# Down product of a gated feed-forward block: seven block products in place of eight, three parts, block sums on GpSimd

## The chip, the cores and the metric

The kernel runs on one core of a Trainium2 chip. Five engines work from queues of their own: PE (TensorE, matmuls), DVE (VectorE), ACT (ScalarE), POOL (GpSimd) and SP (which issues most transfers). The metric is the device time of one execution in microseconds.

## The reference

Two layers of a hybrid diffusion step over 640 tokens (128 of context, 512 latent), width 1024. The change touches only the feed-forward block that ends each layer:

```python
def conv_ffn(h, p):
    u = h @ p['w_up']
    t = u.shape[1]
    pad = CONV_WIDTH // 2
    up = jnp.pad(u, ((0, 0), (pad, pad), (0, 0)))
    w = p['conv_w']
    u = up[:, 0:t] * w[0] + up[:, 1:t + 1] * w[1] + up[:, 2:t + 2] * w[2] + p['conv_b']
    a, gt = u[..., :D_FF], u[..., D_FF:]
    return (a * jax.nn.silu(gt)) @ p['w_down']
...
    x = x + gate_f * conv_ffn(h, p)
```

`w_up` is 1024 x 5632 and `w_down` is 2816 x 1024, all in float32.

## The kernel before

Activations lie with features on the 128 partitions and the 640 tokens along the free dimension, as two halves of 320 columns (`HALF`). Every float32 operand is split in two fp32r numbers: ACT copies it to the high half (`whi` for weights, `hhi`, `ahi` for activations), and a subtraction gives the low half (`wlo`, `hlo`, `alo`). A product takes three passes of matmuls: high by high, high by low, low by high. A tile of 128 output features is therefore 3 x 2 matmuls of 128x320 for each 128 input features.

One plan, `build_plan`, is a list of steps in program order. Each engine walks the same list (`walk`) and emits the steps that concern it, so a step's place in the list is its place in the queue of every engine that takes part. An engine never passes a step that waits. Semaphores such as `hi_ready`, `lo_ready`, `sub_done` and `fm_read` join the engines, and what is counted in them is worked out by `look_back` and `signals`.

Weights come by DMA into one of two slots of `raw` (`load_unit`), ACT makes the high half (`split`, line 1699), DVE the low half (line 2054), and PE multiplies (`feature_tile`, line 1376). There is room for two blocks of `SUB` = 1024 columns in `whi` and `wlo`.

The 22 tiles of the hidden width are done in two parts (`FPARTS`), of 12 and 10. In a part, the up units come first: unit a makes one tile of the value half and one of the gate half, 96 matmuls. Its results go through `up_out` (ACT reads both from PSUM into `va`, `vg`; DVE adds the two outer taps of the convolution, lines 2287 and 2294), and `up_out2`: silu on ACT, product on POOL (line 2367), high half `ahi` on ACT (line 1900), low half `alo` on POOL (line 2370). The queue order in the loop is: first weight block of unit a, `up_out` of unit a-1, first up matmuls, second weight block, `up_out2` of unit a-1, second up matmuls.

Then the down units follow: unit a is one tile of 128 output features, 6 or 5 hidden tiles in each of two blocks of weights, and `down_out` adds the gated result into `xT`, the residual stream (`residual`, line 2243). In the second part of layer 0, ACT also squares `xT` and DVE adds the squares up for the next layer's norm (line 2260). Up units and down units are both hardware loops.

## Time and profile before

| | |
|---|---|
| median of 3 runs | 2582.42 us (2577.47 to 2582.90) |
| profiled execution: its own time | 2577.76 us |
| its span | 2575.1 us |
| PE busy | 2479.7 us, 96% |
| DVE busy | 1370.1 us, 53% |
| ACT busy | 972.6 us, 38% |
| POOL busy | 410.5 us, 16% |

The span goes from the first instruction to the last. A busy share is an average over stages with different limits: the mixers are bound in other ways than the feed-forward block. A row names the line of the kernel, the engine, the operation, and the tile written and the tiles read. Where an engine was idle before a row, square brackets say how long and whose event ended it.

### The profile page before, as it was taken

What the parts mean: (1) busy time and instruction counts of PE and PEld (TensorE: products, weight loads), DVE (VectorE), ACT (ScalarE), POOL (GpSimd) and SP (SyncE); (2) the same over time, 40 slices, a digit from 0 to 9 for tenths busy, and PEclk for the clock granted to TensorE, in tenths of its full rate; (3) what the DMA queues carried; (4) which work ended last, traced back from release to release, by engine and by line L of the source; (5) the groups of instructions that cost most, each with busy time, mean ns of one, the idle gap of its engine ahead of it and who ended that gap; (6) DMA issues with size and microseconds to landing.
All of it is one profiled execution on the core that took longest, in us unless ns stands there. A gap on an engine that the chain in (4) does not pass through costs nothing.

```text
span 2575.1 us, 42771 instructions
## 1 busy us (share of the span) xinstructions
PE 2479.7 (96%) x17115; PEld 2257.8 (88%) x17115; DVE 1370.1 (53%) x2339; ACT 972.6 (38%) x1713; POOL 410.5 (16%) x362
## 2 busy tenths in 40 slices
PE   7999999999999999999999999999999999999998
PEld 5878977798799999999977799668978999999998
DVE  4674366646755454245447734766476555433542
ACT  5453255424533433133244523454244243322332
POOL 0500022023020221022004001220320202200220
PEclk8999999999999999999999999999999999999999
DMA  7312222422042222322332022222210422222222
GB/s 240 98 34 66 60 96 93 132 87 60 19 124 73 66 65 78 86 66 69 103 97 74 18 74 65 93 85 72 79 50 18 132 65 68 75 74 78 80 59 82
DMA packets 252833, 202.80 MB, mean 79 GB/s; under 512 B 9876, under 2 KB 235910, under 8 KB 252678
## 3 DMA queue, kind: packets, MB, share of 16 engines
q1 hardware_dynamic: 245574, 197.67, 25.4%
q10 hardware_dynamic: 7104, 2.95, 0.4%
q8 instruction: 111, 1.82, 0.3%
q14 instruction: 44, 0.36, 0.0%
HBM read 196.50 MB, written 4.10 MB: 78 GB/s over the span
## 4 chain that ended last, share of the span: by engine, by line
PE 88%; ACT 4%; DVE 4%; issue 1%; DMA 1%; SPq 1%; POOL 0%; ACTq 0%; POOLq 0%; DVEq 0%
PE ps L1376 48%; PE ps L1398 8%; PE ps L1547 6%; PE ps L1561 4%; PE ps L1588 4%; PE ps L1361 3%; PE ps L1363 3%; PE ps L1362 3%; ACT prob L1832 2%; PE ps L1488 1%; PE ps L1445 1%; PE ps L1251 1%; PE ps L1505 1%; PE ps L1508 1%; PE ps L1261 1%
## 5 line engine op out<-in xcount | busy, mean ns | idle before, releaser
L2054 DVE TENSOR_TENSOR wlo<-raw,whi 128x1024 fp32r<-128x1024 f32 (+4 forms) x284 | 357.5, 1259 | 434.1 <-ACT whi L1699 432.6
L1376 PE MATMUL ps<-hhi,whi 128*128 128x320 f32 x1856 | 425.2, 310 | 7.5 <-DVE wlo L2054 3.8
L1376 PE MATMUL ps<-hhi,wlo 128*128 128x320 f32 x1856 | 423.5, 309 | 0.0
L1376 PE MATMUL ps<-hlo,whi 128*128 128x320 f32 x1856 | 423.5, 309 | 0.0
L1699 ACT ACTIVATE whi<-raw 128x1024 fp32r<-128x1024 f32 (+4 forms) x284 | 277.7, 978 | 379.0 <-PE ps L1376 294.9
L1376 PEld LDWEIGHTS ps<-hhi,whi 128*128 128x128 f32 x1856 | 310.6, 188 | 9.8 <-DVE wlo L2054 5.1
L1376 PEld LDWEIGHTS ps<-hlo,whi 128*128 128x128 f32 x1856 | 311.0, 188 | 0.0
L1376 PEld LDWEIGHTS ps<-hhi,wlo 128*128 128x128 f32 x1856 | 310.8, 188 | 0.0
L2343 POOL TENSOR_TENSOR rstd<-smean,mhalf 128x4 f32<-128x4 f32 (+3 forms) x96 | 118.7, 1239 | 550.8 <-DVE smean L2104 550.1
L2128 DVE TENSOR_REDUCE negmax<-ps 128x1 f32<-128x640 f32 x192 | 151.8, 821 | 71.7 <-PE ps L1547 70.7
L1398 PE MATMUL ps<-hhi,whi 128*128 128x320 f32 x512 | 177.8, 347 | 0.5 <-issue 0.5
L2367 POOL TENSOR_TENSOR va<-va,vg 128x640 f32<-128x640 f32 x44 | 74.8, 1699 | 636.8 <-ACT vg L1898 636.8
L1832 ACT ACTIVATE prob<-ps,negmax 128x640 f32<-128x640 f32 x192 | 150.5, 792 | 67.2 <-DVE negmax L2128 67.2
L1376 PE MATMUL ps<-ahi,whi 128*128 128x320 f32 x704 | 160.6, 308 | 4.6 <-DVE wlo L2054 3.9
L1376 PE MATMUL ps<-alo,whi 128*128 128x320 f32 x704 | 159.9, 308 | 0.0
L1376 PE MATMUL ps<-ahi,wlo 128*128 128x320 f32 x704 | 159.8, 307 | 0.0
L1398 PE MATMUL ps<-hhi,wlo 128*128 128x320 f32 x512 | 159.2, 311 | 0.0
L1398 PE MATMUL ps<-hlo,whi 128*128 128x320 f32 x512 | 159.1, 311 | 0.0
L1842 ACT ACTIVATE probT<-ps 128x512 f32<-128x512 f32 (+1 forms) x172 | 88.2, 513 | 179.6 <-PE ps L1561 179.6
L1361 PE MATMUL ps<-whi,hhi 128*128 128x512 f32 (+2 forms) x400 | 146.3, 366 | 1.1 <-ACT vC L1736 0.9
L1363 PE MATMUL ps<-whi,hlo 128*128 128x512 f32 (+2 forms) x400 | 144.5, 361 | 0.0
L1362 PE MATMUL ps<-wlo,hhi 128*128 128x512 f32 (+2 forms) x400 | 144.0, 360 | 0.0
(248 smaller groups left out, 4335.9 us busy)
## 6 DMA issues: line engine op xcount, KB each, us to landing
raw<-in_w_up SPq DMA_DIRECT2D x88, 512.0 KB, 4.9
raw<-in_w_in SPq DMA_DIRECT2D x40, 1024.0 KB, 5.2
raw<-in_w_ada SPq DMA_DIRECT2D x29, 1024.0 KB, 5.2
raw<-in_w_down SPq DMA_DIRECT2D x16, 768.0 KB, 4.8
raw<-in_w_down SPq DMA_DIRECT2D x16, 640.0 KB, 4.4
adaw<-in_w_ada SPq DMA_DIRECT2D x8, 1024.0 KB, 11.4
raw<-in_w_o SPq DMA_DIRECT2D x8, 1024.0 KB, 5.5
raw<-in_w_branch_a SPq DMA_DIRECT2D x4, 1024.0 KB, 5.0
```

The lines of the kernel that those rows point to most:

```text
L1361: pe.matmul(out, hhi[:, kt, c], wh, start=kt == 0, stop=False)
L1362: pe.matmul(out, hhi[:, kt, c], wl, start=False, stop=False)
L1363: mm = pe.matmul(out, hlo[:, kt, c], wh, start=False, stop=kt == KD - 1)
L1376: mm = pe.matmul(out, w[:, sub, c], m[:, kt, o:o + HALF], start=first and i == 0 and a == 0, stop=last and i == len(ks) - 1 and a == 2)
L1398: mm = pe.matmul(bank(6)[:, OFF:], w[:, s["sub"], c], m[:, kt, o:o + HALF], start=kt == a == 0, stop=kt == KD - 1 and a == 2)
L1547: mm = pe.matmul(out, qt[:, q * P:(q + 1) * P], kt[:, SEQ + c:SEQ + c + HALF], start=True, stop=True)
L1561: mm = pe.transpose(bank(bk)[:, i * P:(i + 1) * P], src, ident[:, :])
L1699: act.activation(dst(whi), src, ACT.Copy).then_inc(S["hi_ready"], 1)
L1832: act.activation(prob[:, slot + m, :], run(m), ACT.Exp, bias=negmax[:, at], accum_out=sums)\
L2054: dve.tensor_tensor(dst(wlo), src, dst(whi).bitcast(F32), ALU.subtract).then_inc(S["lo_ready"], 1)
L2128: dve.tensor_reduce(negmax[:, slot + m:slot + m + 1], run(m), AX.X, ALU.max, negate=True)\
L2343: pool.tensor_tensor(rstd[:, par, 0:heads], smean[:, par, 0:heads], mhalf[:, 0:heads], ALU.pow)\
```

## The change

Part one: `FPARTS` becomes three parts, of 8, 8 and 6 hidden tiles. Part two: the down product of a part is worked out by Strassen's scheme in Winograd's form, on blocks. A column pair u is 256 output features: its weights are four blocks, A11 and A12 (the first output tile), A21 and A22 (the second), with the first and the second half of the part's hidden tiles. The tokens are in two halves as before. Seven products P1 to P7 replace eight. They take four weight blocks as they are and four block sums, S1 = A21 + A22, S2 = S1 - A11, S3 = A22 - S2 and S4 = A12 - S2 (A11, A12 and A22 serve as they are, A21 only in sums); POOL makes the sums in place in `raw` (`wmix`). On the activation side also, three block sums are made once for a part: `up_out3` takes the place of the end of `up_out2`. It makes high halves on ACT, low halves on DVE, and sums on POOL. An even unit has two copies of 320 columns and one sum, an odd unit two of 640 and one of 320, with two sums. All go to `acts`, which holds seven operands.

Part three: the results. Each product has a PSUM bank of its own for 320 columns, and DVE adds it with the gate straight into the quarters of `xT` that it belongs to (x11, x12 for the first output tile's token halves, x21, x22 for the second's). P1 is copied by ACT to a shared sum in `vg`, to which DVE adds P6 and later P7. Weight blocks are split in quarters of 512 columns (`qsplit`), four products ahead. The steps are written out, no longer in a loop.

```diff
-FPARTS = [(0, 12), (12, 10)]
+FPARTS = [(0, 8), (8, 8), (16, 6)]
+PAIRS = KD // 2
+PRODUCTS = ["P1", "P5", "P2", "P6", "P3", "P7", "P4"]
+WEIGHT = dict(P1="A11", P5="S1", P2="A12", P6="S2", P3="S4", P7="S3", P4="A22")
+PLACE = dict(A11=(0, 0), S3=(0, 0), A21=(0, 1), S1=(0, 1), S2=(0, 1), A12=(1, 0), S4=(1, 0), A22=(1, 1))
+READS = dict(P1=["x11"], P5=["x22", "x12"], P2=["x11"], P6=["U", "x12"], P3=["x12"], P7=["U", "x21", "x22"], P4=["x21"])
+OPERAND = dict(P1=0, P5=1, P2=2, P3=3, P6=4, P7=5, P4=6)
...
+        def load(u):
+            plan.append(dict(step="unit", src="down", slot=u % 2, a=u, of=l, **k))
+
+        def mix(u, name):
+            plan.append(dict(step="wmix", name=name, slot=u % 2, u=u, **k))
...
+        def split(g):
+            u, p = seq[g]
+            name = WEIGHT[p]
+            if name == "A11" and u > 1:
+                mix(u, "S1")
+            plan.append(dict(step="qsplit", name=name, u=u, slot=u % 2, q=g % 4, last=p == "P4", **k))
+            if name == "S1" and u:
+                mix(u, "S2")
+            if name == "A12" and u:
+                mix(u, "S4")
+                mix(u, "S3")
+            if name == "A22" and u + 2 < PAIRS:
+                load(u + 2)
...
+        def product(g):
+            u, p = seq[g]
+            need = 2 + (g > 1) if g < 4 else 1 if g < 8 else ends[g - 8]
+            plan.append(dict(step="prod", p=p, u=u, q=g % 4, bank=(g + 4) % 8, read_back=len(reads) - need,
+                             copy_back=sum(x > g - 8 for x in copies), **k))
...
+        out_v, out_g = [dict(last[2], a=nf - 1, s=1, js=js) for js in ((0,), (1,))]
+        plan.extend(last[:5])
+        load(0)
+        load(1)
+        plan.extend(last[5:7])
+        split(0)
+        mix(0, "S1")
+        plan.append(out_v)
+        split(1)
+        mix(1, "S1")
+        mix(0, "S2")
+        plan.append(last[7])
+        plan.append(out_g)
+        split(2)
+        split(3)
+        adds = []
+        for g in range(len(seq)):
+            u, p = seq[g]
+            product(g)
+            if g == 0:
+                plan.append(dict(last[5], a=nf - 1, s=1))
+            left = [read(g)]
...
+            if squares and p in ("P3", "P4"):
+                left.append(dict(step="down_sq", f=2 * u + (p == "P4"), **k))
+                adds.append(dict(step="down_sq2", f=2 * u + (p == "P4"), **k))
...
+            if g + 4 < len(seq):
+                split(g + 4)
+            if g == 1:
+                plan.append(dict(last[6], a=nf - 1, s=1))
+                mix(0, "S4")
+                mix(0, "S3")
...
+        def mixed(s, out, turn):
+
+            at = ds(turn + s["a"] // 2, 1)
+            a, b = va[:, 0, :].rearrange("p (o c) -> p o c", o=2), va[:, 1, :].rearrange("p (o c) -> p o c", o=2)
+            pieces = [(2, 4, b), (4, 6, a), (6, 7, b[:, 0:1, :])] if s["a"] % 2 else [(0, 1, a[:, 0:1, :]), (1, 2, a[:, 0:1, :])]
+            return [(out[:, i:j, at, :], x.unsqueeze(2)) for i, j, x in pieces]
...
+                def prod(s):
+
+                    p, half = s["p"], s["nf"] // 2
                     sub_waits(s)
-                    half = s["nf"] // 2
-                    if s["first"] and s["sub"] == 0:
-                        pe.wait_ge(S["alo_ready"], n("alo_ready", -half))
-                    fm_waits(s, 1)
-                    feature_tile(2 * s["s"], s["sub"], range(s["sub"] * half, (s["sub"] + 1) * half), P, 0, ahi, alo,
-                                 first=s["sub"] == 0, last=s["sub"] == 1, base=s["sub"] * half,
-                                 made="alo_ready" if s["first"] and s["sub"] else None).then_inc(S["sub_done"], 1)
+                    pe.wait_ge(S["fm_read"], n("fm_read", -s["read_back"]))
+                    pe.wait_ge(S["copy_done"], n("copy_done", -s["copy_back"]))
+                    out, (ah, al) = bank(s["bank"], HALF), operands(s)
+                    wh, wl = quarter(whi, s), quarter(wlo, s)
+                    for k in range(half):
+                        if s["u"] == 0 and k == half - 1:
+                            pe.wait_ge(S["alo_ready"], n("alo_ready", -dict(P1=1, P2=2, P3=2, P6=1, P7=1).get(p, 0)))
+                        c = slice(k * P, (k + 1) * P)
+                        for w, m, a in ((wh, ah, 0), (wh, al, 1), (wl, ah, 2)):
+                            mm = pe.matmul(out, w[:, c], m[:, OPERAND[p], k, :], start=k == a == 0, stop=k == half - 1 and a == 2)
+                    mm.then_inc(S["sub_done"], 1)
...
+                def down_sq(s):
+                    squares(s["f"], s["f"] % 2, -1)
+
+                def down_read(s):
+                    if s["p"] == "P1":
+                        act.wait_ge(S["sub_done"], n("sub_done"))
+                        act.wait_ge(S["fm_read"], n("fm_read", -s["room_back"]))
+                        act.wait_ge(S["prod_ready"], n("prod_ready", -int(s["u"] < 2)))
+                        act.activation(shared_sum(s), bank(s["bank"], HALF), ACT.Copy).then_inc(S["copy_done"], 1)
+
+                def qsplit(s):
+                    if s["name"][0] == "S":
+                        act.wait_ge(S["wmix_ready"], n("wmix_ready", -s["mix_back"]))
+                    else:
+                        act.wait_ge(S[f"raw_full{s['slot']}"], n(f"raw_full{s['slot']}"))
+                    act.wait_ge(S["sub_done"], n("sub_done", s["ahead"] - 1))
+                    act.activation(quarter(whi, s).rearrange("p (k c) -> p k c", c=P), block_of(s, s["name"]), ACT.Copy).then_inc(S["hi_ready"], 1)
...
+                def up_out3(s):
+
+                    act.wait_ge(S["prod_ready"], n("prod_ready"))
+                    for i, (out, src) in enumerate(mixed(s, operands(s)[0], n.turn)):
+                        if i:
+                            act.wait_ge(S["tmix_ready"], n("tmix_ready", i))
+                        act.activation(out, src, ACT.Copy).then_inc(S["ahi_ready"], 1)
...
+                    dve.wait_ge(S["hi_ready"], n("hi_ready", 1))
+                    wh, wl = [quarter(x, s).rearrange("p (k c) -> p k c", c=P) for x in (whi, wlo)]
+                    dve.tensor_tensor(wl, block_of(s, s["name"]), wh.bitcast(F32), ALU.subtract).then_inc(S["lo_ready"], 1)
+
+                def up_out3(s):
+                    ah, al = operands(s)
+                    for i, ((hi, _), (lo, src)) in enumerate(zip(mixed(s, ah, n.turn), mixed(s, al, n.turn))):
+                        dve.wait_ge(S["ahi_ready"], n("ahi_ready", i + 1))
+                        dve.tensor_tensor(lo, src, hi.bitcast(F32), ALU.subtract).then_inc(S["alo_ready"], 1)
...
+                    out = bank(s["bank"], HALF)
+                    total = shared_sum(s)
+                    for i, (op, back) in enumerate(s["ops"]):
+                        if back is not None:
+                            dve.wait_ge(S["fm_read"], n("fm_read", back))
+                        if op == "U":
+                            ins = dve.tensor_tensor(total, total, out, ALU.add)
+                        else:
+                            f, half = 2 * s["u"] + int(op[1]) - 1, int(op[2]) - 1
+                            src = total if p in ("P1", "P6", "P7") else out
+                            for j, (a, b) in enumerate(((0, SEQ), (SEQ, HALF))) if half == 0 else ((1, (HALF, T)),):
+                                x = xT[:, f, a:b]
+                                ins = dve.scalar_tensor_tensor(out=x, in0=src[:, a - half * HALF:b - half * HALF],
+                                                               scalar=mod[:, s["l"], 5 * KD + f, j:j + 1], in1=x,
+                                                               op0=ALU.mult, op1=ALU.add)
+                        ins.then_inc(S["fm_read"], 1)
 
...
-                    pool.wait_ge(S["ahi_ready"], n("ahi_ready", 1))
-                    u = ds(n.turn * 2 + s["a"], 1)
-                    pool.tensor_tensor(alo[:, u, :], a.unsqueeze(1), ahi[:, u, :].bitcast(F32), ALU.subtract)\
-                        .then_inc(S["alo_ready"], 1)
...
+                    if s["a"] % 2 == 0:
+                        pool.wait_ge(S["alo_ready"], n("alo_ready", 1))
+                        pool.tensor_tensor(a[:, 0, :], a[:, 1, :], a[:, 0, :], ALU.subtract).then_inc(S["tmix_ready"], 1)
+                        return
+                    pool.wait_ge(S["alo_ready"], n("alo_ready"))
+                    pool.wait_ge(S["prod_ready"], n("prod_ready"))
+                    pool.tensor_tensor(a, b[:, 1:2, :].to_broadcast([P, 2, HALF]), a, ALU.subtract).then_inc(S["tmix_ready"], 1)
+                    pool.wait_ge(S["tmix_ready"], n("tmix_ready", 1))
+                    pool.wait_ge(S["alo_ready"], n("alo_ready", 1))
...
+                    a, b, op = dict(S1=("A21", "A22", ALU.add), S2=("S1", "A11", ALU.subtract), S3=("A22", "S2", ALU.subtract),
+                                    S4=("A12", "S2", ALU.subtract))[name]
+                    pool.tensor_tensor(block_of(s, name), block_of(s, a), block_of(s, b), op).then_inc(S["wmix_ready"], 1)
```

The order on DVE in a down part. Before, in the down loop of the first part (part of 12), each difference covers 6 hidden tiles, and a residual is two instructions:

```order
L2052 REGISTER_ALU
L2054 TENSOR_TENSOR wlo<-raw,whi 128x768 [waits hi_ready]
L2052 REGISTER_ALU
L2054 TENSOR_TENSOR wlo<-raw,whi 128x768 [waits hi_ready]
L2243 ISA [waits mod_ready,sub_done]
L2243 ISA
L2243 SCALAR_TENSOR_TENSOR xT<-ps,mod,xT 128x128
L2243 ISA
L2243 SCALAR_TENSOR_TENSOR xT<-ps,mod,xT 128x512
L2052 REGISTER_ALU
L2054 TENSOR_TENSOR wlo<-raw,whi 128x768 [waits hi_ready]
```

After, in the first part of layer 0: column pair 0's P3 (one update), P7 (four instructions) and P4 (two) between differences, and the first piece of the next result (`hf<-hf,ps` is the addition to the shared sum, `xT<-hf,mod,xT` takes the shared sum in, `xT<-ps,mod,xT` a bank):

```order
L2238 TENSOR_TENSOR wlo<-raw,whi 128x512 [waits hi_ready]
L2481 SCALAR_TENSOR_TENSOR xT<-ps,mod,xT 128x320 [waits fm_read,mod_ready,sub_done]
L2238 TENSOR_TENSOR wlo<-raw,whi 128x512 [waits hi_ready]
L2475 TENSOR_TENSOR hf<-hf,ps 128x320 [waits fm_read,mod_ready,sub_done]
L2481 SCALAR_TENSOR_TENSOR xT<-hf,mod,xT 128x128 [waits fm_read]
L2481 SCALAR_TENSOR_TENSOR xT<-hf,mod,xT 128x192
L2481 SCALAR_TENSOR_TENSOR xT<-hf,mod,xT 128x320 [waits fm_read]
L2238 TENSOR_TENSOR wlo<-raw,whi 128x512 [waits hi_ready]
L2481 SCALAR_TENSOR_TENSOR xT<-ps,mod,xT 128x128 [waits fm_read,mod_ready,sub_done]
L2481 SCALAR_TENSOR_TENSOR xT<-ps,mod,xT 128x192
L2238 TENSOR_TENSOR wlo<-raw,whi 128x512 [waits hi_ready]
L2481 SCALAR_TENSOR_TENSOR xT<-ps,mod,xT 128x128 [waits fm_read,mod_ready,sub_done]
```

What moved: each block of weights now has a difference of 512 columns, and between two of them stand one to four instructions that take a product in. An update with the shared sum waits for the addition ahead of it by `fm_read`.

The order on POOL at the border from the up loop to the down part. Before, the last two units' product and low half, and then the next up loop:

```order
L2367 TENSOR_TENSOR va<-va,vg 128x640 [waits silu_done]
L2370 TENSOR_TENSOR alo<-va,ahi 128x640 [waits ahi_ready]
L2367 TENSOR_TENSOR va<-va,vg 128x640 [waits silu_done]
L2370 TENSOR_TENSOR alo<-va,ahi 128x640 [waits ahi_ready]
L871 UNCONDITIONAL_BRANCH
```

After, at the same place: the even unit's product and sum, then weight sums (`raw<-raw`), then the last unit's product and its two sums, and the weight sums that follow.

```order
L2574 TENSOR_TENSOR hf<-hf 128x640 [waits silu_done]
L2581 TENSOR_TENSOR hf<-hf 128x320 [waits alo_ready]
L2600 TENSOR_TENSOR raw<-raw 128x4x128 [waits raw_full0]
L2600 TENSOR_TENSOR raw<-raw 128x4x128 [waits raw_full1]
L2600 TENSOR_TENSOR raw<-raw 128x4x128 [waits wmix_ready,lo_ready] x2
L2574 TENSOR_TENSOR hf<-hf 128x640 [waits silu_done]
L2585 TENSOR_TENSOR hf<-hf 128x640 [waits prod_ready,alo_ready]
L2588 TENSOR_TENSOR hf<-hf 128x320 [waits alo_ready,tmix_ready]
L2600 TENSOR_TENSOR raw<-raw 128x4x128 [waits wmix_ready,lo_ready] x4
L2600 TENSOR_TENSOR raw<-raw 128x4x128 [waits raw_full0]
```

What moved: two of the weight sums that wait for low halves stand ahead of the last unit's product, and four more right behind it.

The order on ACT around unit 1's outputs, just ahead of the up loop (the turns of the loop have the same order with register rows between). Before: silu, one high half, and behind the loop's branch the first weight block of the next unit but one:

```order
L1699 ACTIVATE whi<-raw 128x1024 [waits sub_done,raw_full0]
L1898 ACTIVATE vg<-vg 128x640 [waits fm_read]
L1900 ACTIVATE ahi<-va 128x640 [waits prod_ready]
L871 UNCONDITIONAL_BRANCH
L871 ISA
L1697 ISA [waits raw_full1]
L1699 ACTIVATE whi<-raw 128x1024 [waits sub_done]
```

After, from the second weight block on:

```order
L1869 ACTIVATE whi<-raw 128x1024 [waits sub_done,raw_full0]
L2071 ACTIVATE hf<-hf 128x640 [waits fm_read]
L2079 ACTIVATE acts<-hf 128x2x320 [waits prod_ready]
L2079 ACTIVATE acts<-hf 128x2x320 [waits tmix_ready]
L2079 ACTIVATE acts<-hf 128x320 [waits tmix_ready]
L995 UNCONDITIONAL_BRANCH
L995 ISA
L1867 ISA [waits raw_full1]
L1869 ACTIVATE whi<-raw 128x1024 [waits sub_done]
```

What moved: the weight block behind the branch now stands behind three high halves, of which the second and the third wait for POOL's sums (`tmix_ready`).

## Rows read from the trace of the kernel before

**Rows 1.** The page: engines, chain by engine, one group of matmuls (busy us, mean ns | idle).

```profile
PE 2479.7 (96%) x17115; PEld 2257.8 (88%) x17115; DVE 1370.1 (53%) x2339; ACT 972.6 (38%) x1713; POOL 410.5 (16%) x362
...
PE 88%; ACT 4%; DVE 4%; issue 1%; DMA 1%; SPq 1%; POOL 0%; ACTq 0%; POOLq 0%; DVEq 0%
...
L1376 PE MATMUL ps<-ahi,whi 128*128 128x320 f32 x704 | 160.6, 308 | 4.6 <-DVE wlo L2054 3.9
```

**Rows 2.** PE timeline in a down part, and of a gate: start us, us, row.

```profile
637.90 0.31 PE L1398 MATMUL ps<-hhi,wlo 128*128 128x320 f32 x1
638.04 0.31 PE L1398 MATMUL ps<-hhi,whi 128*128 128x320 f32 x1
...
1084.41 0.45 PE L1376 MATMUL ps<-ahi,whi 128*128 128x320 f32 x2
1084.70 0.45 PE L1376 MATMUL ps<-alo,whi 128*128 128x320 f32 x2
```

**Rows 3.** Windows of both feed-forward stages.

```profile
core 0: us, PE busy (x) PEld busy (x) DVE busy (x) ACT busy (x) POOL busy (x), PEclk, DMA share, GB/s
829.30:1315.00 485.70, 480.34 (x3261) 475.93 (x3262) 217.44 (x319) 159.15 (x202) 73.24 (x45) 0.99 0.27 78
2062.00:2573.00 511.00, 502.86 (x3458) 497.33 (x3456) 218.59 (x321) 162.26 (x208) 73.19 (x45) 1.00 0.25 71
```

**Rows 4.** DVE groups by form: count | busy us, mean ns | idle us, releaser.

```profile
L2054 DVE TENSOR_TENSOR wlo<-raw,whi 128x768 fp32r<-128x768 f32 x32 | 33.5, 1046 | 60.8 <-ACT whi L1699 60.8
...
L2235 DVE SCALAR_TENSOR_TENSOR hlo<-merged,hhi 128x640 fp32r<-128x640 f32 x16 | 25.9, 1656 | 0.2
...
L2086 DVE TENSOR_TENSOR stage<-stage,gains 128x512 f32<-128x512 f32 x30 | 20.8, 692 | 1.0
...
L2260 DVE TENSOR_TENSOR hf<-hf,nsq 128x640 f32<-128x640 f32 x19 | 15.6, 821 | 0.6
```

**Rows 5.** DVE timeline in one turn of the up loop, layer 0.

```profile
876.78 1.00 DVE L2287 SCALAR_TENSOR_TENSOR vg<-ps,PT,vg 128x127 f32<-128x127 f32 x2
877.93 1.01 DVE L2294 SCALAR_TENSOR_TENSOR vg<-ps,PT,vg 128x127 f32<-128x127 f32 x2
878.85 1.22 DVE L2054 TENSOR_TENSOR wlo<-raw,whi 128x1024 fp32r<-128x1024 f32 x1
883.36 1.89 DVE L2054 TENSOR_TENSOR wlo<-raw,whi 128x1024 fp32r<-128x1024 f32 x1 [3.29 <-ACT whi L1699]
```

**Rows 6.** POOL groups by form.

```profile
L2370 POOL TENSOR_TENSOR alo<-va,ahi 128x640 f32 x32 | 50.5, 1577 | 34.5 <-ACT ahi L1900 34.5
...
L2337 POOL TENSOR_TENSOR tmps<-stage,ropeh 128x256 f32<-128x256 f32 x24 | 17.6, 734 | 0.0
```

**Rows 7.** POOL timeline in the same turn of the up loop.

```profile
882.59 1.58 POOL L2370 TENSOR_TENSOR alo<-va,ahi 128x640 f32 x1 [1.09 <-ACT ahi L1900]
```

**Rows 8.** Timeline of POOL and DVE at a merge of layer 0.

```profile
526.00 4.09 POOL L2361 TENSOR_TENSOR merged<-merged,gated 128x640 f32<-128x640 f32 x2 [66.74 <-DVE gated L2229]
...
526.57 2.08 DVE L2054 TENSOR_TENSOR wlo<-raw,whi 128x1024 fp32r<-128x1024 f32 x1
```

**Rows 9.** ACT timeline in the same turn of the up loop.

```profile
873.65 0.89 ACT L1891 ACTIVATE va<-ps,PT 128x640 f32<-128x640 f32 x1 [5.10 <-PE ps L1376]
...
881.64 0.74 ACT L1900 ACTIVATE ahi<-va 128x640 f32 x1 [1.93 <-POOL va L2367]
...
882.28 1.04 ACT L1699 ACTIVATE whi<-raw 128x1024 fp32r<-128x1024 f32 x1
```

**Rows 10.** ACT groups by form.

```profile
L1770 ACT ACTIVATE tmpq<-stage 128x384 f32<-128x384 f32 x54 | 28.2, 527 | 2.5 <-DVE smean L2104 1.2
```

**Rows 11.** PE waits at two up-to-down borders: us, times, longest.

```profile
PE ps L1376 <- DVE wlo L2054: 0.6, 1, 0.6
...
PE ps L1376 <- DVE wlo L2054: 1.4, 1, 1.4
PE ps L1376 <- POOL alo L2370: 0.3, 1, 0.3
```

**Rows 12.** The page's DMA issues: KB each, us to landing.

```profile
raw<-in_w_ada SPq DMA_DIRECT2D x29, 1024.0 KB, 5.2
```

194 lines of the change are left out of this document (135 added, 59 removed).

## The prediction, written before the changed kernel was run

> **What bounds the kernel now.** I read the page first. TensorE is busy for 96% of the span, it is 88% of the chain that ended last, and the down products are 3 x 704 of its matmuls [rows 1]. At the granted clock of 1.00 (2.4 GHz) two 128x320 matmuls start every 0.293 us, so one costs 0.1466 us; a stream into one bank with new weights for each matmul, which is the form that the new products have, goes at the same pace (637.90 to 638.04) [rows 2]. The windows of the two feed-forward stages say the same: PE 480 of 486 us, while DVE has 217, ACT 159 and POOL 73 [rows 3]. So fewer matmuls are worth their full time, as long as DVE, which prepares the low halves of all weights and takes the results out of PSUM, keeps up in the down parts and not only on the average of the stage.
>
> **What the change removes.** 2112 down matmuls become 7/8 of that, 1848: 264 x 0.1466 = -38.7 us.
>
> **DVE in a down part.** A part now has 28 products (4 column pairs by 7). Each is 12 matmuls in the parts of 8 (1.76 us) and 9 in the part of 6 (1.32 us): 12.3 and 9.2 us for a column pair. For it DVE has, by the order, 7 weight differences and 15 instructions that take results in. Their price: two taps of 127 and 511 columns start 0.92 us before the next instruction, which is 638 columns at 1.04 ns (0.665; 640 columns take 0.82 and 1024 take 1.22, so 384 more take 0.40) and 0.13 for each instruction [rows 4, 5]. So 320 columns cost 0.46, 128 and 192 together 0.59, a difference of 512 is 0.66 (the row for 512 says 0.69 from start to end), one of 384 is 0.53 [rows 4]. The nine updates of xT are four of 0.59 and five of 0.46, the two additions to the shared sum 0.46 each, and twice the next one waits for such an addition (0.13): 5.8 us. With the differences: 10.5 us in a part of 8 and 9.6 in the part of 6. By itself DVE is under PE in the first (10.5 of 12.3) and above it in the second (9.6 of 9.2). Before, in a part of 12, it had 4 differences of 1.05 and 4 residual instructions for two output tiles, in 144 matmuls or 21 us.
>
> **GpSimd against DVE.** GpSimd adds four block sums for a column pair. 256 columns take 0.73 and 640 take 1.57 [rows 6], so 512 take 1.29 and 384 take 1.01. The two engines get in each other's way here: the difference of 1024 columns takes 1.22 alone, 1.89 when it meets alo on GpSimd (it waited from 883.36 to about 884.17) [rows 5, 7], and 2.08 between two merges, the second of which waited for it in turn (two took 4.09) [rows 8]. xT updates from the shared sum have two SBUF inputs as well; such a form (hlo<-merged,hhi) took 1.66 a piece beside merges, against 0.82 for 640 columns [rows 4]. An update whose source is PSUM is not held up in these rows.
> In a column pair of a part of 8 that gives, counted from the end of difference A12: S4 runs 0.1 to 1.4, and difference S2, due at 0.6, loses 0.65; S3 follows to 3.1, and the first piece of the P1 update loses 1.1; S1 of the next pair comes between the two pieces and takes 1.1 more; S2's sum, released by difference S1, costs P7's update 0.75. Together 3.6: 14.1 us against PE's 12.3. With sums of 1.01 it is 0.35 + 0.85 + 0.85 + 0.45 = 2.5: 12.1 against 9.2. The bounds are nothing lost (10.5 and 9.6) and every sum lost whole (15.7 and 13.6); I take the middle case since it alternates as the two merges did.
> The Trainium skill (SBUF — State Buffer, "SBUF: two separate sides") calls the shared ports an exclusive lock, taken for a whole instruction by a DVE operation with two SBUF inputs or by GpSimd, while the other fully blocks. Our row loses 0.67 of an overlap of 0.81, so a start of 0.13 is hidden; with full blocking the sum below would be some 10 us higher. The Trainium skill (Perfetto Trace Analysis, "Optimizing Scalar/DVE Operations") warns that moving work between these two might not help, which speaks against this change.
>
> **The squares.** In the last part of layer 0, P3 and P4 are each followed by a square on ACT that waits for DVE's update (0.74, as ahi [rows 9]); the high half of the next weight block (0.53 for 384 columns [rows 10]) stands behind it on ACT, and DVE's difference behind that: 1.35 us of idle DVE, twice, and two additions of 640 columns at 0.80. 12.1 becomes 16.4.
>
> **The start of a down part.** After the last up matmul: gate output on ACT and DVE's taps to 3.0, two differences to 4.4, silu to 3.8. GpSimd's queue has S2 of pair 1 ahead of the activation's product (waits for the second difference, to 5.9; the product then ends near 7.75). High half to 8.6; DVE takes it after the first two products' results and two differences, at 10.7; then block sum 12.3, high 13.1, low 13.9, last low half 14.4 (13.9 with 384 columns). Only then come product 2's result and difference 6. From there to the last difference are 22 product turns, and one product follows. Part of 8: 14.4 + 22/7 x 14.1 + 1.8 = 60.5, against 28 x 1.76 = 49.3: +11.2. Part of 6 in layer 1: 13.9 + 38.0 + 1.3 = 53.2, against 36.9: +16.3. In layer 0, with squares: 13.9 + 51.5 + 1.3 = 66.7: +29.8. Four, one and one: +90.9 us.
>
> **The end of a down part.** The next up unit's first difference (1.2) stands behind the results of three products on DVE (1.05, 0.46, 1.64): 4.35 after the last small difference, 1.76 of it beneath the last product: +2.6, four times, 10.4. The way into layer 1 and out to the output has about as much late, 4.5 in all. Before had waits of 0.6 and 1.4 + 0.3 [rows 11] at its up-to-down borders, 4.6 over both layers, which I count as gone into the above. Net +10.3. The loads (1 MB, 5.2 us to landing [rows 12]) have more than a pair's time and stay hidden.
>
> **The up loop.** In before GpSimd makes alo and is done at 884.17; DVE's difference for the next unit follows early. Now an odd unit's chain runs: high half of two blocks to 882.4 as before, DVE's low half to 883.4, GpSimd 885.1 and again 886.0, ACT 886.0 and 886.7, and only then, since it is behind them on ACT, the high half of the next unit's first weight (1.04) to 887.9, DVE to 889.1. A unit is 96 matmuls, 14.1 us; the ACT row at 873.65 is just behind a unit's end, so the next starts about 887.5 [rows 5, 7, 9]. PE waits 1.6 us. This is at three units of a part of 8 and two of the part of 6: 16 times, 26 us. Bounds: 0.9 each where no loop registers delay it, 2.0 each.
>
> **Sum.** -38.7 + 90.9 + 10.3 + 26 = +88.5. The profiled execution took 2577.8 (span 2575.1), which is the lower of the runs; their median is 4.7 higher. 2577.8 + 88.5 = 2666 us.
>
> **The rivals.**
> 1. The sum above, DVE bound by its own work and GpSimd's: 0.53.
> 2. The block sums fall into DVE's pauses, so nothing is lost to them. The start costs 3.5 in a part of 8 and PE binds after it; the parts of 6 cost 7 and, with squares, 20. 4 x 3.5 + 27 + 10 + 26 - 38.7 = +38, 2616. For it: POOL works only 5.2 of 12.3 us. Against it: two sums stand back to back behind a difference. 0.2.
> 3. Faster: the updates hide, DVE is never late but for the borders (6 x 2) and the squares (6): -38.7 + 18 = -21, 2557. This decides if DVE's pair, with what it loses, stays under 9.2 us in the part of 6 and under 12.3 in the others. Its own 9.6 speaks against it. 0.07, and 0.03 for a result within 0.2% (which is about what a measurement of this kernel can tell).
> 4. Each sum costs DVE its whole time: 1.6 and 1.5 more for a pair, 22/7 of these by part, +30: 2696. 0.17.
>
> **Range.** From rival 2 with up stalls of 0.9 (2605) to rival 4 with a little over: 2600 to 2700. Faster 0.07, same 0.03, slower 0.90.
>
> **What would show it.** Right: in a down part DVE busy or held for nearly all the time and PE idle with wlo as releaser, some 1.8 us a column pair in the parts of 8 and 2.9 in the plain part of 6; 512-column differences well above 0.69 beside raw<-raw; down part of 6 in layer 0 near 67 us; PE waiting about 1.6 us at the start of every second up unit. Wrong: DVE's instructions at their undisturbed times with gaps, or the waits put down to GpSimd or a DMA.

## The result, and the profile after

The changed kernel takes 2621.3 us (median of 4 runs, 2617.7 to 2622.8), against 2582.7 for the kernel before on the same chip: a ratio of 1.0156, with a 95% interval of 1.0144 to 1.0169. It is slower by 39 us, where 88 were forecast. The profiled execution took 2617.7 (span 2615.9), 39.9 more than the profiled one of before, and the sums of this section and the table of terms below are made against that pair.

The page of the changed kernel, with the lines that answer to [rows 1]; the products' first matmul group is L1618 now:

```profile
PE 2468.5 (94%) x16851; PEld 2227.0 (85%) x16851; DVE 1637.6 (63%) x2848; ACT 1055.5 (40%) x1907; POOL 542.4 (21%) x480
...
PE 61%; issue 18%; DVE 9%; ACT 5%; POOL 4%; DMA 1%; SPq 1%; POOLq 0%; ACTq 0%; DVEq 0%
...
L1618 PE MATMUL ps<-acts,whi 128*128 128x320 f32 x1232 | 286.3, 320 | 41.6 <-DVE wlo L2238 33.5
```

264 matmuls are gone (17115 to 16851), as the change says, but PE's busy time fell by 11 us only, and PE now waits 42 us at the down products, 33.5 of it for DVE's differences of quarter blocks (L2238). DVE has 268 us more than before, GpSimd 132 more.

Windows of four of the six down parts of the changed kernel with their borders (the two left out are 58.8 and 58.9 long; start to end in us, then PE's busy time and count, and its mean granted clock):

```profile
core 0: us, PE busy (x), PEclk, DMA share, GB/s
942.70:1001.60 58.90, 52.34 (x337) 0.97 0.24 71
...
1260.90:1319.90 59.00, 44.10 (x253) 0.94 0.31 100
2236.80:2295.70 58.90, 52.33 (x338) 0.97 0.24 71
...
2554.50:2603.60 49.10, 41.52 (x253) 0.97 0.10 33
```

The same for layer 0 of the kernel before (layer 1 reads the same within 0.1 us):

```profile
1000.00:1085.40 85.40, 84.79 (x578) 1.00 0.28 80
1226.20:1298.80 72.60, 70.93 (x483) 1.00 0.41 127
```

Further down, a part's time without its border goes from the start of its first matmul to the end of its last one. Added up, the down product takes 343.6 us now and took 316.0. It has 38.7 us less to multiply and is 27.6 longer, so 66 us were given back inside these windows. PE is idle in them for 48.7 us (before 4.6), and busy for 294.9 where 1848 matmuls at 0.1466 are 270.9 (before 311.4 and 309.6): 44 us of waits and 22 of slower matmuls behind them. Not all of the 22 are a lower clock: without block sums (below) a part of 8 is busy for 50.5 us at a clock of 1.00, where its matmuls are 49.3. The up stages add 9.3, and 3 lie outside both.

The beginning of one down part on PE (start us, us, row, and in brackets the idle time before it and what ended it):

```profile
950.79 0.56 PE L1618 MATMUL ps<-acts,whi 128*128 128x320 f32 x2 [0.55 <-DVE wlo L2238]
...
953.50 0.57 PE L1618 MATMUL ps<-acts,whi 128*128 128x320 f32 x2 [1.13 <-DVE acts L2244]
...
958.77 0.56 PE L1618 MATMUL ps<-acts,whi 128*128 128x320 f32 x2 [2.79 <-DVE wlo L2238]
```

The part began at 942.6. Counted from 0 in the order of issue, product 4 starts 0.55 late and waits 1.13 more ahead of its last hidden tile, for the low half of the last up unit's activation (`acts`); product 6 starts 2.79 late. DVE and GpSimd in the same stretch, and at the third column pair:

```profile
947.03 1.73 DVE L2481 SCALAR_TENSOR_TENSOR xT<-hf,mod,xT 128x128 f32<-128x128 f32 x2
948.68 2.05 DVE L2238 TENSOR_TENSOR wlo<-raw,whi 128x512 fp32r<-128x512 f32 x1
...
955.45 1.05 DVE L2244 TENSOR_TENSOR acts<-hf,acts 128x320 fp32r<-128x320 f32 x1 [1.27 <-ACT acts L2079]
956.43 1.68 DVE L2481 SCALAR_TENSOR_TENSOR xT<-hf,mod,xT 128x128 f32<-128x128 f32 x2
958.03 0.68 DVE L2238 TENSOR_TENSOR wlo<-raw,whi 128x512 fp32r<-128x512 f32 x1
...
974.15 1.87 DVE L2481 SCALAR_TENSOR_TENSOR xT<-hf,mod,xT 128x128 f32<-128x128 f32 x3
...
977.14 1.41 DVE L2238 TENSOR_TENSOR wlo<-raw,whi 128x512 fp32r<-128x512 f32 x1
978.47 2.75 DVE L2481 SCALAR_TENSOR_TENSOR xT<-hf,mod,xT 128x128 f32<-128x128 f32 x2
...
987.62 1.87 DVE L2481 SCALAR_TENSOR_TENSOR xT<-hf,mod,xT 128x128 f32<-128x128 f32 x3
```

```profile
947.08 1.46 POOL L2600 TENSOR_TENSOR raw<-raw 128x512 f32<-128x512 f32 x1 [3.15 <-DVE wlo L2238]
...
954.87 2.76 POOL L2600 TENSOR_TENSOR raw<-raw 128x512 f32<-128x512 f32 x2
...
976.71 4.30 POOL L2600 TENSOR_TENSOR raw<-raw 128x512 f32<-128x512 f32 x3 [1.62 <-DVE wlo L2238]
```

A difference of 512 columns (L2238, 0.68 alone) takes 1.41 when GpSimd starts a sum first: by its length alone (1.29) the sum runs from 976.71 to 978.0, and the difference is through 0.5 after it. The next update, two pieces with two SBUF inputs (L2481 xT<-hf), takes 2.75, against 0.67 beside no sum; each piece waits for one of the two sums that follow. Updates whose source is PSUM are not longer beside a sum (0.66 from 976.55 on, with the sum from 976.71). That is the alternation forecast from [rows 8], and the pair from 974.15 to 987.62 loses 0.7 + 2.1 + 0.7 = 3.5 us to it (forecast: 3.6).

### The profile page after: what moved, and what is told of

It is laid out like the page before. It is cut to its first block, busy times and chain, and to the rows that moved or that the text cites. A ratio compares the mean times of both kernels' runs of the same rounds, so it can differ in the third digit from the quotient of the medians.

```text
span 2615.9 us, 43297 instructions
## 1 busy us (share of the span) xinstructions
PE 2468.5 (94%) x16851; PEld 2227.0 (85%) x16851; DVE 1637.6 (63%) x2848; ACT 1055.5 (40%) x1907; POOL 542.4 (21%) x480
## 3 DMA queue, kind: packets, MB, share of 16 engines
q1 hardware_dynamic: 222918, 197.67, 24.6%
## 4 chain that ended last, share of the span: by engine, by line
PE 61%; issue 18%; DVE 9%; ACT 5%; POOL 4%; DMA 1%; SPq 1%; POOLq 0%; ACTq 0%; DVEq 0%
PE ps L1526 18%; PE ps L1548 7%; PE ps L1703 6%; PE ps L1717 4%; PE ps L1744 4%; PE ps L1618 4%; PE ps L1511 3%; PE ps L1513 3%; PE ps L1512 3%; DVE xT L2481 3%; POOL hf L2574 2%; DVE wlo L2238 2%; ACT prob L2002 2%; PE ps L1644 1%; PE ps L1595 1%
## 5 line engine op out<-in xcount | busy, mean ns | idle before, releaser
L2232 DVE TENSOR_TENSOR wlo<-raw,whi 128x1024 fp32r<-128x1024 f32 (+2 forms) x220 | 271.4, 1234 | 223.3 <-ACT whi L1869 222.1
L1618 PE MATMUL ps<-acts,whi 128*128 128x320 f32 x1232 | 286.3, 320 | 41.6 <-DVE wlo L2238 33.5
L1869 ACT ACTIVATE whi<-raw 128x1024 fp32r<-128x1024 f32 (+2 forms) x220 | 227.3, 1034 | 229.0 <-PE ps L1526 128.0
L1618 PEld LDWEIGHTS ps<-acts,whi 128*128 128x128 f32 x1232 | 211.5, 194 | 54.3 <-DVE wlo L2238 44.5
L1618 PE MATMUL ps<-acts,wlo 128*128 128x320 f32 x616 | 193.9, 315 | 0.0
L2244 DVE TENSOR_TENSOR acts<-hf,acts 128x320 f32 (+3 forms) x110 | 88.4, 808 | 140.2 <-ACT acts L2079 138.7
L2574 POOL TENSOR_TENSOR hf<-hf 128x640 f32<-128x640 f32 x44 | 75.1, 1708 | 480.8 <-ACT hf L2071 480.8
L2600 POOL TENSOR_TENSOR raw<-raw 128x512 f32<-128x512 f32 (+1 forms) x96 | 122.4, 1278 | 167.7 <-DVE wlo L2238 156.5
```

The lines of the kernel that those rows point to most:

```text
L1618: mm = pe.matmul(out, w[:, c], m[:, OPERAND[p], k, :], start=k == a == 0, stop=k == half - 1 and a == 2)
L1869: act.activation(dst(whi), src, ACT.Copy).then_inc(S["hi_ready"], 1)
L2232: dve.tensor_tensor(dst(wlo), src, dst(whi).bitcast(F32), ALU.subtract).then_inc(S["lo_ready"], 1)
L2574: pool.tensor_tensor(a, a, vg[:, s["s"], :], ALU.mult).then_inc(S["prod_ready"], 1)
L2600: pool.tensor_tensor(block_of(s, name), block_of(s, a), block_of(s, b), op).then_inc(S["wmix_ready"], 1)
```

## The experiments

Each is compared with the kernel before on the same chip; its own median is given, then the ratio with its interval. The medians of the kernel before differ from set to set (2577.8 to 2582.7 us), so two kernels of different sets are compared by their ratios (0.001 is 2.6 us) or by their traces, not by their medians.

**No block sums.** The changed kernel without GpSimd's sums of weight blocks; the products take unsummed blocks, so the output is not the reference's. ACT's high halves wait for the load in place of the sum.

```diff
-            plan.append(dict(step="wmix", name=name, slot=u % 2, u=u, **k))
```

> The changed kernel with GpSimd's four weight sums of each column pair left out (the blocks are used as they were loaded, so the down result is not the reference's); every product, update and difference stays. Theory A, GpSimd is most of the price (it holds DVE in the pairs, and a weight sum stands ahead of the last unit's activation product at the start of each part): the wait at a part's start shrinks from 5.5 us to about 2, no slow matmuls after it (2.3 us in each part of 8), the parts of 6 lose 4 us each: 6 x 3.5 + 4 x 2.3 + 8 = 38 less, near 2580. Rival B, DVE's own 15 updates and 7 differences are the price and the sums fall into its pauses: 10 less at most, 2608 or above.

2590.4 us, 1.0052 [1.0039, 1.0065]: between the two theories, nearer to A. The sums cost 27 us by the ratios and 29 by the two traces (spans 2586.6 and 2615.9). The windows of one part of 8 and of the plain part of 6, without the sums:

```profile
942.60:995.90 53.30, 50.53 (x338) 1.00 0.27 80
...
2531.80:2575.00 43.20, 38.44 (x254) 1.00 0.11 38
```

A part of 8 takes 53.3 in place of 57.2: product 6 starts 1.9 sooner (956.90), and after it PE never waits, which is worth the other 2.0. The wait at the border falls from 1.8 to 1.1, the parts of 6 from 59.1 and 49.2 to 54.7 and 43.2. Even with sums that cost nothing the kernel is slower than before.

**GpSimd's first product before its sum.** At a part's start the sum S2 of pair 1 stood ahead of the activation's product on GpSimd, which the forecast had named as a delay. Here it stands behind.

```diff
-            if name == "S1" and u:
+            if name == "S1" and u > 1:
                 mix(u, "S2")
...
             if g == 0:
                 plan.append(dict(last[5], a=nf - 1, s=1))
+                mix(1, "S2")
```

> One step moved: sum S2 of column pair 1 goes behind the activation product of the last up unit in GpSimd's queue. Theory A, the queue order on GpSimd sets the start: product 6 starts 2 us earlier in each of six parts, 12 less, and 9 more if PE's clock then stays up after the shorter wait: 2597 to 2606. Rival B, DVE's own queue (results 0 and 1 and differences 4 and 5 ahead of the low halves) sets the start: within 3 us of 2618.

2627.0 us, 1.0193 [1.018, 1.0206]: 9 us slower than the changed kernel, by the ratios and by the traces alike. DVE and GpSimd at the same place:

```profile
946.83 1.79 POOL L2575 TENSOR_TENSOR hf<-hf 128x640 f32<-128x640 f32 x1 [2.72 <-ACT hf L2072]
948.57 1.36 POOL L2601 TENSOR_TENSOR raw<-raw 128x512 f32<-128x512 f32 x1
949.89 1.65 POOL L2586 TENSOR_TENSOR hf<-hf 128x640 f32<-128x640 f32 x1
```

```profile
947.21 2.93 DVE L2482 SCALAR_TENSOR_TENSOR xT<-hf,mod,xT 128x128 f32<-128x128 f32 x2
950.07 2.02 DVE L2239 TENSOR_TENSOR wlo<-raw,whi 128x512 fp32r<-128x512 f32 x1
```

The product comes 1.7 us earlier (946.83 for 948.50), but now three operations of GpSimd follow each other without a gap, and the update at 947.21 takes 2.93 in place of 1.73, since each of its two pieces waits for one. A part takes 57.9 for 57.2. The six parts together are 4 us longer; 3 us lie in two up stages whose start is at half the clock in this trace, and the rest outside both. So the product comes earlier and the part still ends later, and neither theory had that.

**Squares behind.** In the last part of layer 0 the squares on ACT stand behind the high half of the next weight block.

```diff
-                left.append(dict(step="down_sq", f=2 * u + (p == "P4"), **k))
+                sq.append(dict(step="down_sq", f=2 * u + (p == "P4"), **k))
...
             if g + 4 < len(seq):
                 split(g + 4)
+            plan.extend(sq)
```

> Only in the last part of layer 0: the squares on ACT go behind the high half of the next weight block, in place of ahead. As the prediction had it, 1.35 us of idle DVE twice in a pair, 22/7 pairs: 8.5 less. By the trace of the changed kernel, whose turns in this part are 0.45 us longer than in the plain part of 6 (1.96 against 1.51), of which 0.23 are the additions: 5 less. Rival, DVE is bound by the additions and its own work there and the order on ACT does not matter: no change.

2616.7 us, 1.0153 [1.014, 1.0166]. The part falls by 5.5, from 59.1 to 53.6, as the estimate from the trace (5) had it, but the total by less than can be told from nothing: an up stage (115.8 for 114.3) and the stretch between the layers (818.9 for 816.6), which the edit doesn't touch, are longer in this trace. This trace also shows what the granted clock costs in a part of 8. Its two parts of 8 in layer 0:

```profile
943.60:1000.80 57.20, 51.10 (x337) 1.00 0.21 64
1118.40:1175.60 57.20, 52.62 (x337) 0.97 0.21 64
```

One has a clock of 1.00 throughout, the other was at half for a stretch, and both take 57.2 us. In the first, product 6 starts after a wait of 2.80 us; in the second the matmuls ahead of it are slower and the wait is 1.26. Both wait 0.9 and 0.5 for differences later on. DVE's pace sets the part.

**Three parts alone.** The kernel before, eight products, with `FPARTS` of the changed one.

```diff
-FPARTS = [(0, 12), (12, 10)]
+FPARTS = [(0, 8), (8, 8), (16, 6)]
```

> The kernel before with its two parts of 12 and 10 cut in three, of 8, 8 and 6, eight products as it was. Theory A, a further part costs one more border, 0.6 to 1.7 us in a layer, and the loss of the change is all in the new down part: 2579 to 2582. Rival, shorter parts cost by themselves (a fuller share of border work, smaller down blocks on DVE and ACT): 10 us or more, 2588 or above.

2614.0 us, 1.0143 [1.0129, 1.0158]: the rival's side, 36 us, nearly all that the change costs. PE's waits from 842 to 2604 (total, times, longest), and the windows of four of the six parts:

```profile
PE ps L1376 <- DVE wlo L2054: 19.6, 14, 2.9
```

```profile
943.80:1004.10 60.30, 58.20 (x386) 0.97 0.31 88
...
1264.30:1319.20 54.90, 46.85 (x292) 0.94 0.39 123
...
2407.00:2467.30 60.30, 56.91 (x387) 1.00 0.31 87
2551.70:2601.10 49.40, 45.29 (x289) 0.93 0.17 48
```

The six windows add up to 348.2, against 316.0 for four parts with as many matmuls. At each start PE waits 2.1 (parts of 8) or 2.85 (parts of 6) for a difference, where [rows 11] had 0.6 and 1.4, and at four of the six starts 1.3 to 1.7 more for `alo`. PE is idle for 24.2 us in the six windows (before 4.6) and busy 12.5 longer for the same matmuls, at a granted clock of 0.93 to 0.97 in four of the six. 4 us lie outside the windows.

**High halves late.** In the changed kernel's up loop, the activation's high halves of the unit before stand ahead of the next unit's work on ACT, so they no longer precede the high half of a weight block.

```diff
-            if kind == "up":
+            before = [dict(step="up_out3", s=s, a=unit_before - 1, **k)] if kind == "up" and unit_before else []
...
-            return u[:2] + out + u[2:4] + out2 + u[4:]
+            return u[:2] + before + out + u[2:4] + out2 + u[4:]
```

> The changed kernel with the copies and sums of up_out3 moved, in the up loop, behind the next unit's first weight block on ACT, DVE and GpSimd; the down parts are as they were. The up stages of the changed kernel are 9.3 us longer than their matmuls. If the queue order on ACT is the cause, as the prediction had it at 26 us, these 9 go: 2612. Rival, the waits come from DVE's own added work in the up loop, wherever it stands: no change.

The first turn of the loop is written out for it. 2613.0 us, 1.0123 [1.0108, 1.0139], 8 to 9 us less than the changed kernel by the ratios. PE in the first and last up stage of layer 0:

```profile
845.30:943.90 98.60, 98.60 (x674) 1.00 0.26 75
...
1175.00:1259.70 84.70, 84.70 (x577) 1.00 0.24 70
```

PE does not wait in them. Over both layers the up stages are 7.9 us shorter than in the changed kernel, 1.2 above their matmuls. The edit met its expectation: nearly all of the 9.3 us of the up stages were this chain on ACT.

**Sums on DVE.** `wmix` moves from GpSimd to DVE.

```diff
-                    pool.tensor_tensor(block_of(s, name), block_of(s, a), block_of(s, b), op).then_inc(S["wmix_ready"], 1)
+                    dve.tensor_tensor(block_of(s, name), block_of(s, a), block_of(s, b), op).then_inc(S["wmix_ready"], 1)
```

> The four weight sums of each column pair made by DVE in place of GpSimd, at the same places of the plan. Theory A, what GpSimd's sums cost is that they hold DVE's two-input instructions: DVE gains 0.60 us of work for each sum (2.4 in a pair) and loses the 3.4 (parts of 8) that it was held; the starts get 2 us shorter, and PE's clock stays up behind them as without sums (1.7 in each of six parts): 2600 to 2610. Rival B, DVE's own work is the bound: 2.4 x 22/7 = 7.5 more in each part of 6 and 3 in each part of 8: 2640 or above.

2622.1 us, 1.0161 [1.0148, 1.0175]: no difference to the changed kernel, and both theories missed. DVE's groups in the feed-forward stage of layer 0 (count | busy us, mean ns), with the sums on DVE and then as changed:

```profile
L2238 DVE TENSOR_TENSOR wlo<-raw,whi 128x512 fp32r<-128x512 f32 x56 | 38.2, 684 | 0.1
...
L2256 DVE TENSOR_TENSOR raw<-raw 128x512 f32<-128x512 f32 x32 | 24.6, 768 | 1.8 <-DVE raw L2256 0.5
...
L2493 DVE SCALAR_TENSOR_TENSOR xT<-hf,mod,xT 128x128 f32<-128x128 f32 x24 | 12.3, 512 | 0.4
...
L2256 DVE TENSOR_TENSOR raw<-raw 128x384 f32<-128x384 f32 x16 | 10.2, 638 | 0.7
L2493 DVE SCALAR_TENSOR_TENSOR xT<-hf,mod,xT 128x192 f32<-128x192 f32 x24 | 9.9, 412 | 0.0
```

```profile
L2238 DVE TENSOR_TENSOR wlo<-raw,whi 128x512 fp32r<-128x512 f32 x56 | 48.4, 867 | 0.0
...
L2481 DVE SCALAR_TENSOR_TENSOR xT<-hf,mod,xT 128x128 f32<-128x128 f32 x24 | 22.1, 922 | 0.8 <-ACT hf L1840 0.3
...
L2481 DVE SCALAR_TENSOR_TENSOR xT<-hf,mod,xT 128x192 f32<-128x192 f32 x24 | 15.2, 635 | 0.0
```

DVE takes on 24.6 + 10.2 = 34.8 us of sums, and gets back 10.2 + 9.8 + 5.3 in these three groups, 25 us, then 1.8 in the differences of 384 and 2.9 in the low halves of 320 columns (`acts`, mean 492 ns for 730). So GpSimd's sums had taken from DVE over four fifths of what they cost it to do itself. What is left shows mainly in the part with squares (63.1 for 59.1), where the clock is also at half for 17 us, so the two are not separated.

**Three edits.** Sums on DVE, high halves late, squares behind, together.

> Three edits of the changed kernel together: weight sums on DVE, squares behind the next weight block, up_out3 behind the next unit's first weight block. If they act in different stages, their effects add: -15 for the sums, -5.5 for the squares (the measured shortening of that part), -9 for the up loop: near 2590, still above the kernel before. If each only uncovers the next wait, less than half of that: above 2605.

2609.9 us, 1.0108 [1.0093, 1.0124]. The side of the second theory: the parts of 8 stay at 57.3, and only the up stages and the squares come down.

**Three parts, block first.** Three parts and eight products; the second weight block of the first down unit is prepared ahead of the last up unit's output.

```diff
-        plan.extend(u[:2] + list(early) + before[:1] + u[3:4] + before[1:] + list(between) + [u[2], u[4]])
+        first, rest = (before[:1], before[1:]) if kind != "down" else ([], before)
+        plan.extend(u[:2] + list(early) + first + u[3:4] + rest + list(between) + [u[2], u[4]])
```

> The kernel before with three parts (2614) and the second weight block of the first down unit split ahead of the last up unit's outputs, on ACT and DVE. Theory A, the short first block (4 tiles, 3.5 us of matmuls) no longer covers DVE's taps and difference (a wait of 2.1 to 2.85 us in each part): the waits for wlo go, the outputs come 1.3 later and give that back where alo was waited for: 6 to 14 less, 2600 to 2608. Rival, the price of three parts lies elsewhere (further borders, the units of the last part): within 3 us of 2614.

2624.1 us, 1.017 [1.0152, 1.0188]: 7 us slower than three parts alone, which neither theory had. PE's waits for `alo`:

```profile
PE ps L1377 <- POOL alo L2371: 28.5, 6, 5.9
```

The difference is there in time, and PE waits 4.2 to 5.9 for `alo` at each of six starts. So the first wait is only traded for a longer one: the order of the weight blocks alone is not what three parts pay for. The chain of the last up unit's output is: value and gate on ACT (from 941.5 in this trace), taps on DVE, silu, product, high half, low half (to 951.2), 10 us, and it stands at six borders now, ahead of parts whose first unit is shorter.

**Before, value first.** The kernel before with that chain shortened: the value half of the last up unit's output is made ahead of that unit's second block, as the changed kernel orders it.

```diff
+        js = dict(js=(1,)) if kind == "up" else {}
-        return [dict(step=kind + "_out", s=1, a=n - 1, **k), dict(step=kind + "_out2", s=1, a=n - 1, **k)]
+        return [dict(step=kind + "_out", s=1, a=n - 1, **js, **k), dict(step=kind + "_out2", s=1, a=n - 1, **k)]
+
+    def value_first(kind, n, u, k):
+        return u[:-1] + [dict(step="up_out", s=1, a=n - 1, js=(0,), **k)] + u[-1:] if kind == "up" else u
```

> The kernel before, with one thing moved: at each border from the up loop to the down product, the value half of the last up unit's output is made ahead of that unit's second block, as the changed kernel orders it. Theory (the chain of the last up unit's output sets the border): the border waits of the kernel before, 4.6 to 6.2 us over the run, go: 2575 to 2578 us, ratio about 0.998. Rival (something else sets the border): within 2 us of the kernel before.

2572.3 us, 0.9972 [0.9962, 0.9982]: the theory's side, and faster than both kernels. Its down parts of layer 0 (those of layer 1 are 84.5 and 70.7):

```profile
996.80:1081.20 84.40, 84.40 (x578) 1.00 0.29 81
1222.00:1292.70 70.70, 70.70 (x484) 1.00 0.42 130
```

They add up to 310.3, all of it matmuls at full clock; before had 316.0.

**Three parts, value first.** The same edit in the run with three parts.

> The kernel before in three parts (as in the run with three parts alone, 2614 us), with the value half of the last up unit's output made ahead of that unit's second block. Theory (the chain of that output is what three parts pay for at six borders): each border's waits shrink by some 2.8 us, and with them what they bring behind: 2595 to 2600 us. Rival (three parts pay elsewhere): 2610 us or more.

2603.5 us, 1.0095 [1.0081, 1.0108], between the two theories: 12 us less than three parts alone by the ratios (12.7 by the traces), not 14 to 19. Against the two-part kernel with the same edit (0.9972) three parts still cost 32 us (30 by the traces), so the chain explains about a third of their price, and most of it stays with the chain shortened in both. The start of a part of 8 now waits 1.3 for `alo` alone, that of a part of 6 waits 0.9 and 2.3, a part of 8 takes 58.4 (one 60.1), and the six windows add up to 336.3. In the last part of layer 0 each of five later units waits 0.65 for a difference, here as in three parts alone, which the plain part of 6 doesn't have.

**Changed, two edits.** The changed kernel with high halves late and squares behind, sums on GpSimd.

> The changed kernel with both edits that each took time off their own stage, sums left on GpSimd: the last output's high halves late (9 us fewer in the up stages) and the squares behind (5.5 us fewer in one down part). Theory (they add up): 2606 us. Rival (they overlap, or slow clock takes one back): 2610 us or more, as with the sums on DVE (2609.93).

2612.7 us, 1.0133 [1.0116, 1.0149]: the rival's side, no better than the high halves alone. In its trace three up stages without a wait in their course are longer than their matmuls; one of them:

```profile
1172.60:1258.90 86.30, 86.28 (x578) 0.98 0.24 68
```

86.3 at a clock of 0.98, where the run with high halves late had 84.7 at 1.00. PE had waited 1.8 us at the border ahead of it; at another border the same wait (ending at 1000.5) was followed by a stage at 1.00. So 1.6 us here or there are not the edit's.

**No sums, two edits.** The same without block sums; the products take unsummed blocks.

> The changed kernel with the weights' block sums left out (the products take unsummed blocks in their places, the output isn't the reference's), and with both edits that took time off their own stage: the last output's high halves late, the squares behind. So it has the seven products for nothing but what they ask of VectorE and of the start. Theory (the edits add to the run without sums, 2590.4 us): 9.3 us off the up stages and 4 off one down part, 2577 us, level with the kernel before: even free sums only win back what three parts cost. Rival (slower clock behind the waits that are left takes it back): 2583 us or more.

2577.3 us, 0.9991 [0.9981, 1.0001], as the theory had it. The down parts add up to 309.0. With these two edits in place the sums cost 37 us (1.0133 against 0.9991), and without them 27: the prices of the edits don't add up.

## Why the prediction was right in its direction and more than twice too high

Terms in us, by the profiled executions; a part is measured against its matmuls' time:

| term | forecast | measured |
|---|---|---|
| 264 matmuls less | -38.7 | -38.7 |
| four parts of 8 | +44.8 | +31.2 |
| part of 6, plain | +16.3 | +12.3 |
| part of 6, squares | +29.8 | +22.2 |
| border down to up, four | +10.4 | +7.5 |
| up loops | +26.0 | +9.3 |
| layer's border and output | +4.5 | +2.3 |
| waits of before that go | -4.6 | -6.2 |
| sum | +88.5 | +39.9 |

Starts and ends are read to 0.1 us, part by part. By the windows further up, the down terms come to 27.6 and not 28.3, and 3.0 are left for the layer's border and the output.

**The up loop** is the largest miss (-16.7), and a failed step. "DVE's low half to 883.4, GpSimd 885.1 and again 886.0": it put both of GpSimd's sums of an odd unit behind the low half of that same unit. The trace has the first of them right behind the product:

```profile
891.79 1.71 POOL L2574 TENSOR_TENSOR hf<-hf 128x640 f32<-128x640 f32 x1 [10.60 <-ACT hf L2071]
893.65 1.58 POOL L2585 TENSOR_TENSOR hf<-hf 128x640 f32<-128x640 f32 x1
895.99 0.88 POOL L2588 TENSOR_TENSOR hf<-hf 128x320 f32<-128x320 f32 x1 [0.76 <-DVE acts L2244]
```

It ends at 895.23, and only the short sum (L2588) waits for DVE's low half. The 1.6 us of the first sum go from the chain, and some of it comes back, since the low half beside that sum takes 1.35. From the product's end (893.5) to the end of the next unit's difference (899.7) the chain takes 6.2 us, where the forecast had 7.5 (881.6 to 889.1). PE's wait there was 0.1 to 0.4 in place of 1.6, and with slower matmuls behind it a time cost 0.6 on average, sixteen times. That the rest is the order on ACT is shown (high halves late).

**DVE's turn in a down part** was the right mechanism with a size too large, and the parts of 8 are the second large miss (-13.6). The last low half came 13.9 us after the part's start (forecast 14.4). The 22 turns took 40.5 (956.43 to 996.9) where 44.3 were forecast, 12.9 a pair for 14.1. What follows a difference started 0.60 after it, not 0.66, so DVE's own work is 10.1 a pair. The loss to GpSimd is 3.5 where all meetings occur, as computed, but two of the pairs lose 2.5: of one the third sum waited for its block from memory, and the last has no successor. Applying one pair's loss to all was the error; the mean is 12.9 - 10.1 = 2.8. So DVE is above PE's 12.3 by 0.6 us a pair, not by 1.8 as the forecast's sign of being right had it. The last product followed 2.9 after the last difference, not 1.8, since PE was already behind. In the plain part of 6 the pair took 11.0 for 12.1, by the same error; that part's last low half came after 12.8 us, not 13.9. The rival in which PE binds after the start (part of 8 at +3.5) is out: without sums the part is at 53.3, +4.0, and with them at 57.2.

**The squares**: ACT's delay of DVE was 1.22 (forecast 1.35) and the additions 0.73 each (0.80), yet the part was only 9.9 above the plain one, not 13.5. Between the last low half and the last difference there are six of each, 11.7 us. DVE's differences and updates lose 4.4 us to GpSimd's sums in this part and 6.6 in the plain one, counted as their lengths above the undisturbed ones, so some of the sums run in DVE's pauses and 2.2 us come back. That leaves 9.5 of the 9.9.

**Borders** were 1.8 (forecast 2.6).

**Rival 2** had +38, and the measured +39.9 is beside it by luck. Its terms were not what happened: nothing lost to the sums (27 to 29 us), 3.5 at a part of 8 (7.8), 26 in the up loop (9.3).

**The share that was priced nowhere by itself** is the number of parts. The start was counted in each term, but against the matmuls' time and not against what the eight products would pay in three parts. The runs show it: three parts alone cost 36 us, 24 with the shorter output chain that the change brings with it. With parts and chain alike (1.0095 against 1.0156), the seven products with their sums are 0.6% or 16 us slower than eight. On PE they win 38.7. By the ratios the sums cost 27 (1.0156 to 1.0052), and then the orders on ACT, in the up loop and at the squares, 16 (1.0052 to 0.9991). What is left is 27 us under three parts with eight products, so 12 of the 38.7 are lost even then. The two traces place them: 5.7 in the four parts of 8, nearly all at their starts, 4.0 at the borders behind them (1.3 each, where eight products have one such wait), 1.9 in the parts of 6. So each of three causes (parts, sums, the order of the activation's high halves) had a run of its own.

**GpSimd's lock.** The Trainium skill (SBUF — State Buffer, "SBUF: two separate sides") has a DVE operation with two SBUF inputs and a GpSimd operation block each other for a whole instruction. The trace agrees up to a hidden start of 0.13 (sum to 978.0 by its length alone, difference of 0.68 through at 978.55). The warning of the Trainium skill (Perfetto Trace Analysis, "Optimizing Scalar/DVE Operations") that work moved between the two might not help came out: the ratio is 1.0156 with the sums on GpSimd and 1.0161 with them on DVE.

What stays open: why the clock falls after some waits of 1.1 to 2.9 us and not after others of the same length, and how much of the result with the squares behind is that. No run takes apart the 32 us that three parts cost with the chain shortened in both; by the traces 26 lie in the down parts. No kernel with seven products in two parts was tried.

## What to carry to other kernels

Before a product is traded for sums, price what makes the trade possible as a change of its own: here cutting the work in three parts cost 36 us against 39 for the whole change, and one run of the old kernel with the new cut shows it. Moving elementwise work with two SBUF inputs from DVE to GpSimd takes most of its time from DVE again when the two meet; cost it per meeting, pair by pair, not by the worst pair. At a border between stages look for the whole chain of the last output: ordering its first half earlier was the one edit that beat the kernel before.

## What the runs showed of the hardware

The granted clock after short waits. Windows of PE around the wait of 2.79 us in the changed kernel:

```profile
956.00:959.00 3.00, 0.23 (x1) 1.00 0.00 0
959.00:962.00 3.00, 3.00 (x14) 0.56 0.00 0
962.00:966.00 4.00, 4.00 (x27) 0.90 0.82 262
```

PE worked at 2.4 GHz until 956, did little for 3 us, and then had a mean of 0.56 for 3 us and 0.90 for 4 although it was busy throughout (1.00 again from 966 on). Both means are one stretch at 1.2 GHz: in PE's rows from 959.32 to 961.66 two matmuls take 0.68 to 0.73 us, and from 963.05 on 0.45 again. In the kernel before all down windows are at 1.00; in the changed one all six are at 0.94 to 0.97. In its parts of 8 that cost nothing, as DVE was the bound there. Nor did it with eight products: in the run with three parts the two parts of 8 shown are busy for 58.20 and 56.91 us at 0.97 and 1.00, and both take 60.30, as the second waits 1.28 for `alo` where the first is still multiplying. It does cost in an up stage, where PE does not wait: 86.30 at 0.98 against 84.70 at 1.00.

DVE and GpSimd, alternating, slow each other by the piece: an update with two SBUF inputs, written as two pieces, lost one GpSimd operation for each piece when several followed back to back (2.75 and 2.93 against 0.67 alone), and 1.68 when it met only one. The same form from PSUM kept its 0.66 (from 976.55, beside the sum that started at 976.71).
